# Moving compressed outputs, copies, splits and block sums in the engines' orders of an attention layer

## The chip, the cores and the metric

The kernel runs on one core of a Trainium2 chip. The metric is the device time of one execution in microseconds (us), the median of several. Engines are named as in the profile: PE (TensorE), DVE (VectorE), ACT (ScalarE), POOL (GpSimd), SP (the queue that issues the transfers).

## What is computed

A decoder trunk of two layers over 256 tokens of width 2048, all in float32. Layer 0 mixes with a gated convolution and a gated delta rule. Layer 1, where the change lies, is a sparse attention with 16 query heads in 4 groups of key and value heads:

```python
q, k_c, v_c, k_s, v_s, k_w, v_w, gates = _split_cols(x @ w_in, NSA_WIDTHS)
k_cmp = compress_blocks(kv_heads(k_c), cmp_pos_k, cmp_w1_k, cmp_w2_k)   # blocks of 32, stride 16
v_cmp = compress_blocks(kv_heads(v_c), cmp_pos_v, cmp_w1_v, cmp_w2_v)   # gelu(blocks @ w1) @ w2
...
o = gt[..., 0:1] * o_cmp + gt[..., 1:2] * o_slc + gt[..., 2:3] * o_win
return o @ w_out
```

With 256 tokens there are 15 compressed blocks per group, the selected blocks are all blocks, and the window holds all earlier tokens. Each of the three branches is a softmax over its own keys. After each mixer and each feed-forward network (SwiGLU) comes a layer norm of the scaled residual.

## The kernel before

**Weights.** A float32 product is made of three passes of a reduced type: high by high, high by low and low by high (`passes`, lines 1856 to 1858). So every piece of weights is loaded (`raw`), copied and rounded on ACT (`w_hi`, line 640), subtracted on DVE (`w_lo`, line 1134) and then used by PE. A piece of 128x1024 is called a half. `halves(n)` on ACT and on DVE does the next n of them. There are 4 slots (`HL_SLOTS`): ACT can write half h only after PE has used half h-4, DVE follows ACT, and PE follows DVE. ACT, DVE and PE each run a list of work written out by hand, in which `halves` and the other work alternate; each engine takes its list strictly in order.

**Compressing stage.** PE computes the projections `kc` (8 halves), `gates` (2), `vc` (8), then `w1` for keys (8) and for values (8). Per half PE needs some 2.9 us in the projections and 1.45 us in `w1`. ACT copies the projection out of PSUM into `kcT` (line 983). DVE builds the 32-token blocks with the position embedding (`block_sum(b)`, 8 additions, line 1648), rounds them (`block_hi`, line 1652) and subtracts (`block_lo`, line 1655); PE multiplies them by `w1`. DVE also reduces the rotary angles (lines 1628 to 1636) and mirrors the tables (1671, 1672).

**Attention stage.** For each group g (0 to 3) and token tile t (0, 1) PE does `scores` (one block of 15 columns per head, line 2309, and the selected and window scores, line 2318), `probs_T` (transposes the probabilities, line 2083), `outputs` (the compressed outputs `co`, line 2336, then `po` for the two other branches, line 2345) and `heads_out` (transposes the merged heads, name `oT`). In between `fill(n)` does n halves of the next query projection, or, once those are used up, of the output projection (`out_halves`, whose left side is made by `early_split` on ACT, line 659, and DVE, line 1164). `queries(g)` transposes the rotated queries (line 2278).

ACT does `exps` (lines 1031, 1038), the copies of the transposed probabilities in `probs_T` (1046, 1051), `rope_stage` (1009) and `heads_out` (866). DVE does `rope` (1699 to 1704), `put_T` (copies transposed queries, 1710), the masked scores and their maxima in `scores` (1737 to 1751), `masked`, `weights`, and `branches` (weighs and sums co and po out of PSUM, 1776 and 1778).

**PSUM banks.** All these small results share banks 4 to 7. `K[name]` numbers the uses in the order in which they are listed by `uses`, and the bank is `4 + K[name] % 4`. Before PE writes use k, it waits until the use k-4 has been read:

```python
            def sp_use(name, i=None, per=0):
                k = K[name]
                if k >= 4:
                    pe.wait_ge(sp_free[k % 4], at(k // 4, i, per // 4))
                return bank[4 + k % 4]
```

The read that frees `co` and each `po` is that of DVE in `branches`; the one that frees the queries' banks is `put_T`; the transposed probabilities and `oT` are freed by ACT.

Of the kernel before, what the change touches and what calls it, by code (L numbers as in the profile page):

```python
# [77 lines left out]
def trunk(nc, x_in, positions, ln_mix_g, ln_mix_b, ln_ffn_g, ln_ffn_b, ffn_w_in, ffn_w_out,  # L78
# [6 lines left out]
    with ctx:  # L85
# [172 lines left out]
        hT_ready = sem("hT_ready")  # L258
        bank_whole, xT_ready, yt_by_act, yt_by_dve = sem("bank_whole"), sem("xT_ready"), sem("yt_by_act"), sem("yt_by_dve")
# [46 lines left out]
        def outputs_use(g, t):  # L306
            uses([("co", g, t)] + [("po", g, t, b) for b in range(2)])
# [3 lines left out]
        for g in range(NG):  # L311
            scores_use(g, 1)
            if g:
                uses([("oT", g - 1, 1)])
            probs_use(g, 0)
            outputs_use(g, 0)
            uses([("oT", g, 0)])
            probs_use(g, 1)
            if g < NG - 1:
                uses([("q", 2 * g + 2 + a) for a in range(2)])  # L320
                scores_use(g + 1, 0)
            outputs_use(g, 1)
# [302 lines left out]
        def _(act):  # L625
# [342 lines left out]

            halves(3)
            keep_values(0, C["vs"])  # L970
            for n, kv in enumerate(("kc", "vc")):
                if n:
                    halves(2)
                    c = C["gates"]
                    act.activation(gates_out, chunk_in(c)[0][:, 0:SEQ], ACT.Copy).then_inc(pair_free[c % 2], 1)
                halves(8)
                if n:
                    wait_sp(act, ("gates",))
                    act.activation(gates, last_cols(("gates",), 3 * NH), ACT.Sigmoid).then_inc(sp_free[K[("gates",)] % 4], 1)
                c = C[kv]  # L980
                b = chunk_in(c)
                for a in range(2):
                    ins = act.activation(kcT[:, n, 2 * a:2 * a + 2, :], b[a][:, :].rearrange("p (f t) -> p f t", f=2), ACT.Copy)
                ins.then_inc(pair_free[c % 2], 1)
                if n == 0:
                    rotary_tables()
# [7 lines left out]
            for b in range(2):  # L994
                if b:
                    halves(3)
                    put_hT(("kh",))
                    halves(5)
                else:
                    halves(8)  # L1000
                c = C["w1"] + b
                sums = chunk_in(c)[0][0:NCG, 0:CMPH]
                act.activation(cmp_h[0:NCG], sums, ACT.Gelu_apprx_tanh).then_inc(pair_free[c % 2], 1)
# [58 lines left out]
            for g in range(NG):  # L1062
                exps(g, 1)
                halves(1)
                if g:
                    heads_out(g - 1, 1)
                probs_T(g, 0)
# [5 lines left out]
                if g < NG - 1:  # L1073
                    rope_stage(C["q"] + g + 1, FA[("rope", g)])
                if g == NG - 2:
                    for kt in range(4):
                        early_split("out1", kt)
                heads_out(g, 0)
                halves(1)
                probs_T(g, 1)  # L1080
                if g == NG - 2:
                    for kt in range(4, 8):
                        early_split("out1", kt)
                halves(1)
                if g < NG - 1:
                    exps(g + 1, 0)
                halves(2)
# [12 lines left out]
        def _(dv):  # L1100
# [521 lines left out]
            halves(1)  # L1622
# [3 lines left out]
            for r, n in rows:  # L1626
# [10 lines left out]
                if n.start == 0:  # L1637
                    own(ins)
            to_act(ins)
            halves(5)  # L1640
            def block_sum(b):

                chunk_staged(C["vc" if b else "kc"])
                for hf in range(2):
                    lo = slice(16 * hf, 16 * hf + 16)
                    for g in range(NG):
                        src = kcT[:, b, g, 16 * hf:16 * hf + 16 * NCMP].rearrange("p (n l) -> p l n", l=16)
                        ins = dv.tensor_tensor(blk_sum[:, lo, g * NCMP:(g + 1) * NCMP], src, over(posT[:, b, lo], NCMP), ALU.add)
                own(ins)

            def block_hi(b):
                own(dv.tensor_copy(blk_hi[b][:, 0:blk_n], yt_flat[:, 0:blk_n]))

            def block_lo(b):
                dv.tensor_tensor(blk_lo[b][:, 0:blk_n], yt_flat[:, 0:blk_n], blk_hi[b][:, 0:blk_n].bitcast(F32), ALU.subtract)\
# [6 lines left out]
            block_sum(0)  # L1662
            block_hi(0)
            block_lo(0)
            halves(2 + 8)
# [7 lines left out]
            block_sum(1)  # L1673
            halves(2)
            block_hi(1)
# [113 lines left out]
            halves(3)  # L1789
            turned_q(0)  # L1790
            scores(0, 0)
# [3 lines left out]
            for g in range(NG):  # L1795
# [8 lines left out]
                halves(2)  # L1804
                if g == NG - 2:
                    for kt in range(2):
                        early_split("out1", kt)
                if g < NG - 1:
                    rope(C["q"] + g + 1)
                if g == NG - 2:  # L1810
                    for kt in range(2, 4):
                        early_split("out1", kt)
                halves(1)
                if g == NG - 2:
                    for kt in range(4, 8):
# [6 lines left out]
                if g < NG - 1:  # L1822
                    masked(g + 1, 0)
                    weights(g + 1, 0)
                halves(2)
# [8 lines left out]
        def _(pe):  # L1834
# [496 lines left out]
            def outputs(g, t):  # L2331
# [5 lines left out]
                sp_done(ins, name)  # L2337
                for br in range(2):
# [42 lines left out]
            for g in range(NG):  # L2381
# [5 lines left out]
                fill(1)  # L2387
                outputs(g, 0)
# [4 lines left out]
                if g < NG - 1:  # L2393
                    queries(g + 1)
                    scores(g + 1, 0)
# [52 lines left out]
```

## Time and profile before

| | us |
|---|---|
| median of 3 runs | 2419.82 (2419.26 to 2423.41) |
| the profiled execution | 2425.94 |
| its span, first to last instruction | 2424.2 |
| PE busy in it | 2368.8 |
| DVE busy | 1563.2 |
| ACT busy | 1126.5 |

The span lies 1.7 us below the profiled execution's own time, and that execution took 6.1 us more than the median of the other runs. A busy PE is counted from matmul to matmul with modelled ends, so its share says little of its rate. The mean granted TensorE clock was 0.995 of full speed. The compressing stage lies at 1264 to 1345 us of the span, the attention stage at 1437 to 1630 us.

### The profile page before, as it was taken

What the parts mean: (1) busy time and instruction counts of PE and PEld (TensorE: products, weight loads), DVE (VectorE), ACT (ScalarE), POOL (GpSimd) and SP (SyncE); (2) the same over time, 40 slices, a digit from 0 to 9 for tenths busy, and PEclk for the clock granted to TensorE, in tenths of its full rate; (3) what the DMA queues carried; (4) which work ended last, traced back from release to release, by engine and by line L of the source; (5) the groups of instructions that cost most, each with busy time, mean ns of one, the idle gap of its engine ahead of it and who ended that gap; (6) DMA issues with size and microseconds to landing.
All of it is one profiled execution on the core that took longest, in us unless ns stands there. A gap on an engine that the chain in (4) does not pass through costs nothing.

```text
span 2424.2 us, 32228 instructions
## 1 busy us (share of the span) xinstructions
PE 2368.8 (98%) x12361; PEld 2028.6 (84%) x12361; DVE 1563.2 (64%) x2101; ACT 1126.5 (46%) x1516; POOL 29.6 (1%) x69
## 2 busy tenths in 40 slices
PE   8999999999999999999999999999999999999998
PEld 8999988778888888888879888787888888888886
DVE  6657775577666666655587666766766666666556
ACT  4345554564444444444465445545444444444443
POOL 1000000100000000000000000000000000000000
PEclk9999999999999999999999999999999999999999
DMA  7555521645555555655545652335555555555553
GB/s 263 191 174 174 172 105 55 257 161 193 198 195 193 190 191 191 225 191 194 196 164 180 241 174 87 102 122 195 176 196 195 189 198 190 190 210 207 192 194 115
DMA packets 180090, 437.99 MB, mean 181 GB/s; under 512 B 7232, under 2 KB 19632, under 8 KB 165920
## 3 DMA queue, kind: packets, MB, share of 16 engines
q1 hardware_dynamic: 177984, 425.75, 50.7%
q0 software_dynamic: 2016, 11.02, 1.2%
q8 instruction: 59, 0.97, 0.2%
q14 instruction: 31, 0.25, 0.0%
HBM read 434.64 MB, written 2.10 MB: 180 GB/s over the span
## 4 chain that ended last, share of the span: by engine, by line
PE 90%; DVE 5%; ACT 3%; issue 1%; DMA 0%; SPq 0%; DVEq 0%; ACTq 0%
PE bank L1856 28%; PE bank L1857 28%; PE bank L1858 28%; PE bank L2108 2%; PE bank L2345 1%; DVE w_lo L1134 1%; ACT w_hi L640 1%; PE bank L2318 1%; PE bank L2083 1%; DVE stats L1211 1%; DVE x L1210 1%; DVE spare_lo L1134 0%; PE bank L2336 0%; ACT yt L714 0%; DVE yt L1234 0%
## 5 line engine op out<-in xcount | busy, mean ns | idle before, releaser
L1134 DVE TENSOR_TENSOR w_lo<-raw,w_hi 128x1024 fp32r<-128x1024 f32 x776 | 944.6, 1224 | 733.7 <-ACT w_hi L640 731.7
L640 ACT ACTIVATE w_hi<-raw 128x1024 fp32r<-128x1024 f32 x776 | 820.0, 1060 | 1075.7 <-PE bank L1858 1066.6
L1856 PE MATMUL bank<-w_hi,xt_hi 128*128 128x512 f32 x1904 | 748.2, 393 | 2.5 <-DVE xt_lo L1242 1.2
L1858 PE MATMUL bank<-w_hi,xt_lo 128*128 128x512 f32 x1904 | 743.2, 390 | 0.0
L1857 PE MATMUL bank<-w_lo,xt_hi 128*128 128x512 f32 x1904 | 743.1, 390 | 0.0
L1856 PEld LDWEIGHTS bank<-w_hi,xt_hi 128*128 128x128 f32 x1904 | 358.9, 188 | 77.1 <-issue 1.9
L1858 PEld LDWEIGHTS bank<-w_hi,xt_lo 128*128 128x128 f32 x1904 | 358.6, 188 | 75.0
L1857 PEld LDWEIGHTS bank<-w_lo,xt_hi 128*128 128x128 f32 x1904 | 359.0, 189 | 73.2
L1856 PE MATMUL bank<-xt_hi,w_hi 128*128 128x256 f32 x928 | 267.4, 288 | 9.8 <-DVE w_lo L1134 9.8
L1856 PE MATMUL bank<-w_hi,a_hi 128*128 128x512 f32 x672 | 261.7, 390 | 2.1 <-DVE a_lo L1184 2.1
L1857 PE MATMUL bank<-xt_lo,w_hi 128*128 128x256 f32 x928 | 263.4, 284 | 0.0
L1858 PE MATMUL bank<-xt_hi,w_lo 128*128 128x256 f32 x928 | 263.3, 284 | 0.0
L1857 PE MATMUL bank<-w_lo,a_hi 128*128 128x512 f32 x672 | 261.5, 389 | 0.0
L1858 PE MATMUL bank<-w_hi,a_lo 128*128 128x512 f32 x672 | 261.5, 389 | 0.0
L1856 PEld LDWEIGHTS bank<-xt_hi,w_hi 128*128 128x128 f32 x928 | 178.9, 193 | 12.2 <-issue 9.6
L1857 PEld LDWEIGHTS bank<-xt_lo,w_hi 128*128 128x128 f32 x928 | 178.9, 193 | 2.0 <-issue 1.9
L1858 PEld LDWEIGHTS bank<-xt_hi,w_lo 128*128 128x128 f32 x928 | 178.9, 193 | 0.0
L1331 DVE STREAM_TRANSPOSE big<-yt 32x256 f32<-32x256 f32 x352 | 153.5, 436 | 10.0
L1856 PEld LDWEIGHTS bank<-w_hi,a_hi 128*128 128x128 f32 x672 | 126.1, 188 | 29.3 <-DVE a_lo L1184 3.0
L1858 PEld LDWEIGHTS bank<-w_hi,a_lo 128*128 128x128 f32 x672 | 126.1, 188 | 26.1
L1857 PEld LDWEIGHTS bank<-w_lo,a_hi 128*128 128x128 f32 x672 | 126.1, 188 | 26.0
L762 ACT ACTIVATE yt<-bank 128x512 f32<-128x512 f32 x44 | 23.9, 596 | 43.5 <-PE bank L1858 43.5
(277 smaller groups left out, 1489.7 us busy)
## 6 DMA issues: line engine op xcount, KB each, us to landing
raw<-in_ffn_w_in_dram SPq DMA_DIRECT2D x176, 1024.0 KB, 4.9
raw<-in_ffn_w_out_dram SPq DMA_DIRECT2D x88, 1024.0 KB, 4.8
raw<-in_hy_w_in_dram SPq DMA_DIRECT2D x53, 1024.0 KB, 4.9
raw<-in_nsa_w_in_dram SPq DMA_DIRECT2D x41, 1024.0 KB, 5.0
raw<-in_hy_w_out_dram SPq DMA_DIRECT2D x16, 1024.0 KB, 4.9
raw<-in_nsa_w_out_dram SPq DMA_DIRECT2D x16, 1024.0 KB, 5.1
raw<-in_hy_w_in_dram SPq DMA_DIRECT2D x8, 512.0 KB, 8.6
raw<-in_cmp_w_k_dram SPq DMA_DIRECT2D x4, 1024.0 KB, 5.8
```

The lines of the kernel that those rows point to most:

```text
L640: act.activation(weights_of(h)[0], half_of(h), ACT.Copy).then_inc(w_hi_ready, 1)
L1134: dv.tensor_tensor(lo, half_of(h), hi.bitcast(F32), ALU.subtract).then_inc(w_lo_ready, 1)
L1210: own(dv.scalar_tensor_tensor(v, v, ALPHA, acc_bank(n, t, c)[:, :], ALU.mult, ALU.add))
L1211: ins = dv.bn_stats(stats[:, t, c, :], v)
L1331: ins = dv.transpose(dst, src)
L1856: pe.matmul(dst, l_hi, r_hi, start=start, stop=False, skip_group_check=shared)
L1857: pe.matmul(dst, l_hi, r_lo, start=False, stop=False, skip_group_check=shared)
L1858: return pe.matmul(dst, l_lo, r_hi, start=False, stop=stop, skip_group_check=shared)
L2083: ins = pe.transpose(b[0:rows, h * P:(h + 1) * P], src, ident[:, :])
L2108: ins = pe.matmul(b[:, h * P:(h + 1) * P], lhs(h), rhs(h), start=True, stop=True)
L2318: ins = pe.matmul(b[:, h * kn:(h + 1) * kn], qT[:, 4 * g + hp * k + h, v], ksT[:, br, g, 0:kn], start=True, stop=True)
L2345: ins = pe.matmul(b[:, h * P:(h + 1) * P], pT_buf[br][:, k, h * P:(h + 1) * P], vs[:, br, k, g * DH:(g + 1) * DH], start=k == 0, stop=k == t)
```

## The change

On PE, `compressed_out` becomes a function of its own. For t = 0 it stays ahead of `outputs`; for t = 1 and g < 3 it is issued after `queries(g + 1)` and ahead of `scores(g + 1, 0)`, and its place in the numbering of bank uses moves with it. On ACT, `probs_T(0, 0)` goes ahead of `exps(0, 1)`, `heads_out(2, 0)` ahead of the early splits, and those come in groups of 2, 2 and 4 instead of 4 and 4, the last after `exps(3, 0)`. ACT takes over the rounding `block_hi` from DVE, with two new semaphores. On DVE, halves are placed earlier around the rotary angles, the queries' copy and the block sums; the sums for the values are cut in two, with a half of weights between; and the early splits move behind `rope` and behind `weights(3, 0)`.

```diff
--- before.py
+++ after.py
@@ -256,6 +256,7 @@
         xt_hi_ready, xt_lo_ready = sem("xt_hi_ready"), sem("xt_lo_ready")
         stage_free, silu_done = sem("stage_free"), sem("silu_done")
         hT_ready = sem("hT_ready")
+        blk_ready, blk_hi_ready = sem("blk_ready"), sem("blk_hi_ready")
         bank_whole, xT_ready, yt_by_act, yt_by_dve = sem("bank_whole"), sem("xT_ready"), sem("yt_by_act"), sem("yt_by_dve")
         ident_ready, out_ready = sem("ident_ready"), sem("out_ready")
         out_by_pool = sem("out_by_pool")
@@ -304,7 +305,7 @@
             uses([("cT", g, t)] + [("pT", g, t, b, k) for b in range(2) for k in range(t + 1)])
 
         def outputs_use(g, t):
-            uses([("co", g, t)] + [("po", g, t, b) for b in range(2)])
+            uses([("co", g, t)] * (t == 0 or g == NG - 1) + [("po", g, t, b) for b in range(2)])
 
         uses([("q", a) for a in range(2)])
         scores_use(0, 0)
@@ -317,7 +318,7 @@
             uses([("oT", g, 0)])
             probs_use(g, 1)
             if g < NG - 1:
-                uses([("q", 2 * g + 2 + a) for a in range(2)])
+                uses([("q", 2 * g + 2 + a) for a in range(2)] + [("co", g, 1)])
                 scores_use(g + 1, 0)
             outputs_use(g, 1)
         uses([("oT", NG - 1, 1)])
@@ -966,11 +967,17 @@
                     ins = act.activation(vs[:, n, t, :], b[t][:, :], ACT.Copy)
                 ins.then_inc(pair_free[c % 2], 1)
 
+            def block_hi(b):
+
+                act.wait_ge(blk_ready, b + 1)
+                act.activation(blk_hi[b][:, 0:blk_n], yt_flat[:, 0:blk_n], ACT.Copy).then_inc(blk_hi_ready, 1)
+
             halves(3)
             keep_values(0, C["vs"])
             for n, kv in enumerate(("kc", "vc")):
                 if n:
                     halves(2)
+                    block_hi(0)
                     c = C["gates"]
                     act.activation(gates_out, chunk_in(c)[0][:, 0:SEQ], ACT.Copy).then_inc(pair_free[c % 2], 1)
                 halves(8)
@@ -997,7 +1004,9 @@
                     put_hT(("kh",))
                     halves(5)
                 else:
-                    halves(8)
+                    halves(3)
+                    block_hi(1)
+                    halves(5)
                 c = C["w1"] + b
                 sums = chunk_in(c)[0][0:NCG, 0:CMPH]
                 act.activation(cmp_h[0:NCG], sums, ACT.Gelu_apprx_tanh).then_inc(pair_free[c % 2], 1)
@@ -1060,11 +1069,15 @@
             exps(0, 0)
             halves(1)
             for g in range(NG):
-                exps(g, 1)
-                halves(1)
                 if g:
+                    exps(g, 1)
+                    halves(1)
                     heads_out(g - 1, 1)
-                probs_T(g, 0)
+                    probs_T(g, 0)
+                else:
+                    probs_T(g, 0)
+                    exps(g, 1)
+                    halves(1)
                 halves(1)
                 if g == NG - 1:
                     for kt in range(8, EARLY["out1"]):
@@ -1072,18 +1085,21 @@
                 halves(2)
                 if g < NG - 1:
                     rope_stage(C["q"] + g + 1, FA[("rope", g)])
+                heads_out(g, 0)
                 if g == NG - 2:
-                    for kt in range(4):
+                    for kt in range(2):
                         early_split("out1", kt)
-                heads_out(g, 0)
                 halves(1)
                 probs_T(g, 1)
                 if g == NG - 2:
-                    for kt in range(4, 8):
+                    for kt in range(2, 4):
                         early_split("out1", kt)
                 halves(1)
                 if g < NG - 1:
                     exps(g + 1, 0)
+                if g == NG - 2:
+                    for kt in range(4, 8):
+                        early_split("out1", kt)
                 halves(2)
             heads_out(NG - 1, 1)
             late_halves("out1", KT)
@@ -1619,7 +1635,7 @@
             for j in range(4):
                 halves(1)
                 residual(1, j)
-            halves(1)
+            halves(3)
 
             dv.wait_ge(nsa_in, 16 * 6)
             rows = [(slice(0, P), slice(0, 2)), (slice(0, NCG), slice(2, 3))]
@@ -1636,22 +1652,23 @@
                 ins = dv.scalar_tensor_tensor(tv, av, -1.0, av, ALU.mult, ALU.max)
                 if n.start == 0:
                     own(ins)
+                    halves(2)
             to_act(ins)
-            halves(5)
-            def block_sum(b):
+            halves(1)
+
+            def block_sum(b, hf):
 
                 chunk_staged(C["vc" if b else "kc"])
-                for hf in range(2):
-                    lo = slice(16 * hf, 16 * hf + 16)
-                    for g in range(NG):
-                        src = kcT[:, b, g, 16 * hf:16 * hf + 16 * NCMP].rearrange("p (n l) -> p l n", l=16)
-                        ins = dv.tensor_tensor(blk_sum[:, lo, g * NCMP:(g + 1) * NCMP], src, over(posT[:, b, lo], NCMP), ALU.add)
-                own(ins)
-
-            def block_hi(b):
-                own(dv.tensor_copy(blk_hi[b][:, 0:blk_n], yt_flat[:, 0:blk_n]))
+                lo = slice(16 * hf, 16 * hf + 16)
+                for g in range(NG):
+                    src = kcT[:, b, g, 16 * hf:16 * hf + 16 * NCMP].rearrange("p (n l) -> p l n", l=16)
+                    ins = dv.tensor_tensor(blk_sum[:, lo, g * NCMP:(g + 1) * NCMP], src, over(posT[:, b, lo], NCMP), ALU.add)
+                if hf:
+                    ins.then_inc(blk_ready, 1)
 
             def block_lo(b):
+
+                dv.wait_ge(blk_hi_ready, b + 1)
                 dv.tensor_tensor(blk_lo[b][:, 0:blk_n], yt_flat[:, 0:blk_n], blk_hi[b][:, 0:blk_n].bitcast(F32), ALU.subtract)\
                   .then_inc(for_pe, 1)
 
@@ -1659,10 +1676,11 @@
             for b in range(2):
                 for v in (blk_hi[b], blk_lo[b]):
                     dv.tensor_scalar(v[:, blk_n:blk_w], ones[:, 0:blk_w - blk_n], 0.0, None, ALU.mult)
-            block_sum(0)
-            block_hi(0)
+            block_sum(0, 0)
+            block_sum(0, 1)
+            halves(2)
             block_lo(0)
-            halves(2 + 8)
+            halves(5)
 
             dv.wait_ge(from_act, 20)
             n_from[0] = 20
@@ -1670,9 +1688,10 @@
             for cv, sv in ((cosb, sinb), (cosc[0:NCG].unsqueeze(1), sinc[0:NCG].unsqueeze(1))):
                 own(dv.tensor_copy(cv[:, :, 0:hd], cv[:, :, hd:]))
                 own(dv.tensor_scalar(sv[:, :, 0:hd], sv[:, :, hd:], -1.0, None, ALU.mult))
-            block_sum(1)
-            halves(2)
-            block_hi(1)
+            halves(4)
+            block_sum(1, 0)
+            halves(1)
+            block_sum(1, 1)
             halves(2)
             block_lo(1)
             halves(4)
@@ -1786,8 +1805,9 @@
             def turned_q(g):
                 put_T(K[("q", 2 * g)], lambda a: qT[:, 4 * g + 2 * a:4 * g + 2 * a + 2, :])
 
-            halves(3)
+            halves(2)
             turned_q(0)
+            halves(1)
             scores(0, 0)
             masked(0, 0)
             weights(0, 0)
@@ -1802,17 +1822,14 @@
                     for kt in range(8, EARLY["out1"]):
                         early_split("out1", kt)
                 halves(2)
+                if g < NG - 1:
+                    rope(C["q"] + g + 1)
                 if g == NG - 2:
                     for kt in range(2):
                         early_split("out1", kt)
-                if g < NG - 1:
-                    rope(C["q"] + g + 1)
+                halves(1)
                 if g == NG - 2:
                     for kt in range(2, 4):
-                        early_split("out1", kt)
-                halves(1)
-                if g == NG - 2:
-                    for kt in range(4, 8):
                         early_split("out1", kt)
                 halves(1)
                 if g < NG - 1:
@@ -1822,6 +1839,9 @@
                 if g < NG - 1:
                     masked(g + 1, 0)
                     weights(g + 1, 0)
+                if g == NG - 2:
+                    for kt in range(4, 8):
+                        early_split("out1", kt)
                 halves(2)
             mark().then_inc(gb_free, 1)
             late_halves("out1", KT)
@@ -2328,13 +2348,15 @@
                         p_ = sc_buf[t][br][:, 0:HPG * kn].rearrange("p (h n) -> p h n", h=HPG)
                         transposes(("pT", g, t, br, k), [p_[:, h, k * P:(k + 1) * P] for h in range(HPG)])
 
-            def outputs(g, t):
+            def compressed_out(g, t):
                 name = ("co", g, t)
                 wait_sp_read(pe, ("cT", g, t))
                 b = sp_use(name)
                 for h in range(HPG):
                     ins = pe.matmul(b[:, h * P:(h + 1) * P], pT_cmp[0:NCMP, h * P:(h + 1) * P], vcmp[0:NCMP, g, :], start=True, stop=True)
                 sp_done(ins, name)
+
+            def outputs(g, t):
                 for br in range(2):
                     name = ("po", g, t, br)
                     for k in range(t + 1):
@@ -2385,6 +2407,7 @@
                 fill(1)
                 probs_T(g, 0)
                 fill(1)
+                compressed_out(g, 0)
                 outputs(g, 0)
                 fill(2)
                 heads_out(g, 0)
@@ -2392,6 +2415,8 @@
                 fill(2)
                 if g < NG - 1:
                     queries(g + 1)
+                compressed_out(g, 1)
+                if g < NG - 1:
                     scores(g + 1, 0)
                 outputs(g, 1)
                 fill(2 if g < NG - 1 else 1)
```

## Rows read from the trace of the kernel before

**Rows 1.** The page, busy time of the engines.

```profile
PE 2368.8 (98%) x12361; PEld 2028.6 (84%) x12361; DVE 1563.2 (64%) x2101; ACT 1126.5 (46%) x1516; POOL 29.6 (1%) x69
```

**Rows 2.** Timeline of PE, compressing stage: start, duration, line, operation, [idle before, releaser].

```profile
1296.48 0.39 PE L1856 MATMUL bank<-xt_hi,w_hi 128*128 128x256 f32 x1 [1.09 <-DVE w_lo L1134]
...
1323.64 0.38 PE L1856 MATMUL bank<-w_hi,blk_hi 128*128 128x256 f32 x1 [2.29 <-DVE w_lo L1134]
...
1331.44 0.39 PE L1856 MATMUL bank<-w_hi,blk_hi 128*128 128x256 f32 x1 [1.20 <-DVE w_lo L1134]
```

**Rows 3.** Timeline of DVE and ACT, compressing stage.

```profile
1287.91 4.00 DVE L1648 TENSOR_TENSOR yt<-big 128x240 f32<-128x240 f32 x8 [1.20 <-ACT big L983]
...
1291.94 1.16 DVE L1652 CAST blk_hi<-yt 128x1920 fp32r<-128x1920 f32 x1
...
1293.13 2.16 DVE L1655 TENSOR_TENSOR blk_lo<-yt,blk_hi 128x1920 fp32r<-128x1920 f32 x1
1295.21 4.62 DVE L1134 TENSOR_TENSOR w_lo<-raw,w_hi 128x1024 fp32r<-128x1024 f32 x4
...
1318.13 2.95 ACT L640 ACTIVATE w_hi<-raw 128x1024 fp32r<-128x1024 f32 x3
```

**Rows 4.** Timeline of PE and DVE around the first two query transposes.

```profile
1446.87 1.03 PE L2309 MATMUL bank<-big 128*128 128x15 f32 x8 [0.68 <-DVE big L1710]
...
1486.17 1.04 PE L2309 MATMUL bank<-big 128*128 128x15 f32 x8 [0.99 <-DVE big L1710]
...
1489.02 1.15 PE L2336 MATMUL bank<-big 15*128 15x128 f32 x8
...
1490.10 3.84 PE L2345 MATMUL bank<-big,gb 128*128 128x128 f32 x32
1490.28 0.69 DVE L1751 TENSOR_REDUCE sm<-gb 128x4 f32<-128x512 f32 x1
...
1490.88 1.12 DVE L1776 TENSOR_SCALAR big<-bank,sm 128x128 f32<-128x128 f32 x4
...
1493.70 0.48 PE L1856 MATMUL bank<-w_hi,xt_hi 128*128 128x512 f32 x1
```

**Rows 5.** Group 0, tile 0: a window (busy time by engine), then the timeline.

```profile
1456.20:1463.40 7.20, 7.20 (x39) 6.02 (x40) 4.86 (x7) 5.46 (x25) 0.00 (x0) 1.00 0.00 0
...
1464.85 1.15 PE L2336 MATMUL bank<-big 15*128 15x128 f32 x8 [0.86 <-ACT big L1046]
...
1466.73 1.23 DVE L1134 TENSOR_TENSOR w_lo<-raw,w_hi 128x1024 fp32r<-128x1024 f32 x1 [1.15 <-ACT w_hi L640]
1467.88 1.12 DVE L1776 TENSOR_SCALAR big<-bank,sm 128x128 f32<-128x128 f32 x4
...
1474.94 1.04 PE L2083 MATMUL bank<-ident,big 128*128 128x128 f32 x8
```

**Rows 6.** Timeline of PE and DVE in group 2, where the early splits lie.

```profile
1566.13 0.68 DVE L1699 TENSOR_TENSOR yt<-yt 128x512 f32<-128x512 f32 x1
...
1566.97 0.63 PE L2083 MATMUL bank<-ident,sc_more 128*128 128x128 f32 x4 [1.23 <-ACT big L866]
...
1568.27 0.72 PE L2083 MATMUL bank<-ident,sc_more 128*128 128x128 f32 x4 [0.68 <-ACT big L1046]
1568.68 0.74 PE L1856 MATMUL bank<-w_hi,xt_hi 128*128 128x512 f32 x1
...
1569.93 0.75 DVE L1164 TENSOR_TENSOR xt_lo<-big,xt_hi 128x256 fp32r<-128x256 f32 x2
```

**Rows 7.** Windows: stretch, length, busy PE, PEld, DVE, ACT, POOL; granted clock, DMA share, GB/s.

```profile
1319.00:1323.00 4.00, 2.35 (x20) 2.14 (x19) 3.97 (x8) 3.14 (x4) 0.00 (x0) 1.00 0.02 4
...
1466.00:1470.00 4.00, 4.00 (x20) 3.86 (x20) 3.23 (x9) 1.65 (x2) 0.00 (x0) 0.57 0.79 266
...
1564.00:1568.00 4.00, 2.37 (x20) 1.87 (x18) 3.12 (x7) 3.97 (x9) 0.00 (x0) 1.00 0.78 262
1568.00:1572.00 4.00, 3.73 (x12) 3.05 (x13) 3.97 (x8) 3.35 (x9) 0.00 (x0) 0.59 0.00 0
```

## The prediction

> **What bounds the kernel now.** I read the page first. PE is busy for 2368.8 of 2424.2 us [rows 1], and DVE and ACT have room over the whole span. So the end is set by PE, and an edit counts by what it does to the moments in which PE stands still. The list of PE's waits, then the timeline of the two stages that are edited, show where these are. In the compressing stage PE waits for low halves three times for more than 1 us [rows 2], and once more, at 1327.1, for 0.4: 5.0 us together. In the attention stage it waits before the scores of each group until DVE has copied the transposed queries: 0.68 us for group 0, 0.99 for group 1 [rows 4], and 0.99 and 1.00 for groups 2 and 3. It waits 0.86 us for ACT ahead of `co` of group 0, tile 0 [rows 5], and 0.67 us in groups 0 and 1, 1.91 in group 2 [rows 6] and 0.35 in group 3 in the middle of `probs_T(g, 1)`. That is 12 us of standing still in all that the change can work on, 0.5% of the time. Outside these stages nothing is edited.
>
> The second thing to see is the granted clock. It falls to 1.2 of 2.4 GHz twice in the attention stage: from about 1466.3 and from 1568.7, for some 3.4 us each, in which one matmul of 512 columns follows the other after 0.43 instead of 0.23 us [rows 6, 7]. Before the first lie the wait of 0.86 and matmuls of 15 rows, before the second 1.9 us of waits. So such a spell costs up to 1.7 us of PE's time, beyond the waits themselves.
>
> **Compressing stage, keys.** Before, DVE did 8 sums (4.0 us), `block_hi` (1.16) and `block_lo` (2.16) in one piece and only then the low half for which PE had been waiting for 1.09 us [rows 2, 3]. Now two halves stand between the sums and `block_lo`, `block_hi` is ACT's, and the halves k5 to c0 (half 5 of `kc` to half 0 of `vc`; w and n stand below for those of `w1` of the keys and of the query projections) are done around the angles (about 5.3 us of small instructions, for which DVE has the time: each of these halves is still ready at least 1 us before PE comes to it). The needed half ends at about 1293.2 and PE reaches it at 1295.3: the wait goes, -1.1 us.
>
> **Compressing stage, values.** This is where ACT's new work bites. An ACT copy of 1024 columns takes 0.98 us when the next follows at once [rows 3], so one of 1920 takes 0.98 x 1920 / 1024 = 1.84. I go through the order with PE 1.1 us earlier. ACT copies w3, w4, w5 from 1317.0 to 1320.0, then waits for the second half of the sums. DVE: w3 at 1318.05 (1.155 each, [rows 3]), four sums (2.0) until 1321.2, w4, four sums until 1324.35, w5 until 1325.5. ACT rounds from 1324.4 to 1326.2, and behind it in its queue stands w6, which the order of before had copied at 1321.5: ready at 1327.3. DVE w6 until 1328.45, `block_lo` 2.06 until 1330.5, w7 until 1331.75. PE waits for w4 (0.6), w5 (1.7), w6 (1.5) and w7 (1.7), and starts w7 at 1331.8. Before, it started w7 at 1331.44 [rows 2]. So the 1.1 gained is given back and 0.35 more: **+0.35 for the stage**. From there PE needs 1.45 us a half and DVE 1.16, so no more is lost. Bounds: -1.1 if ACT's copy were no obstacle, +2 if the clock also falls over the four waits; the row at 1319 to 1323, with 2.35 of 4.00 us busy, shows no fall behind it [rows 7], so I leave that out of the sum.
>
> **Start of the heads.** `turned_q(0)` now comes one half earlier and the 0.68 us go: -0.7. `probs_T(0, 0)` on ACT is now ahead of `exps(0, 1)`, so `co` starts without the 0.86. But `exps(0, 1)` (5.46 us of ACT's time in its window, [rows 5], 5.3 if all inputs are there) then ends at about 1466.4 instead of 1463.4, and n15 and n16, the halves behind it, 3.1 us later. DVE has both in front of `branches(0, 0)`. Before, it waited 1.15 us between the two [rows 5]; that slack goes and the branches start at 1469.7 instead of 1467.88. They end 3.45 us later, 1473.2, and only then can PE transpose the heads. Before, PE did that at 1474.94. PE itself would be there at 1471.6, without the wait and with the full clock; it stands still for 1.7 us. Result: 1473.3, which is -1.65 with the -0.7 in it, and -0.1 from the next wait: **-1.75 us**. Bounds: -0.7 (the rest lost, by a fall of the clock) to -3.3 (no wait for the branches).
>
> **Compressed outputs, three times.** Before, `co` (4 products, 1.08 us) followed the scores; now it stands in the 0.99 us for which PE waits for the copied queries. That by itself would be worth 0.99 each. But its bank use moves too. In the new order the uses are q, q, co, c, s, s, po, po: `co` is number i+2, and the first `po` is number i+6, the same bank. The first `po` may therefore be written only after DVE has read `co`, and DVE's list has that behind all of `scores(g + 1, 0)`: the last maximum at 1490.28, the four products by the weights 1490.88 to 1492.00 [rows 4]. These times depend on the copied queries and the scores, which are not earlier than before, since c must still wait for `put_T` until 1486.17. In the order of before the bank of the first `po` was that of c, free since 1487.5, and PE started it at 1490.10. Now it starts at 1492.05, after standing still from 1489.0: +1.95 net of the gap filled, and the 3.6 us of po, the weights halves and all that follows on PE move with it [rows 4]. Three groups: **+5.85 us**. Bounds: -3.0 (if the bank did not bind) to +5.9.
>
> **Early splits in group 2.** Counting from the start of PE's `heads_out(2, 0)`, ACT now frees the oT bank first, so the wait of 1.23 goes; then two splits (0.66) and a half (0.98) delay the copy of the compressed probabilities, and the wait of 0.68 becomes 1.3. DVE does `rope` first, 3.8 us (1566.13 to 1569.93, [rows 6]), and the splits that the next fill needs end at 5.6 us from that start, where PE began the fill at 4.85 (1568.68). So +0.75 if the clock falls again, and -0.85 if it does not, because the fill then takes 5.6 instead of 7.2 us: I take **+0.3**. The four splits moved behind `weights(3, 0)` feed fills that PE reaches more than 5 us later; they cost nothing, and would cost DVE's 1.4 us if that cover were gone. The order of `rope` ahead of them hides behind PE's fill.
>
> **The clock.** Each of the three new waits keeps PE idle for 3.0 us at a stretch, more than the 1.9 us before the fall at 1568.7 [rows 7]. I expect a fall behind two of the three, at up to 1.7 us, the price that the rows show: **+3.3 us**, with 0 and 5 as bounds. The Trainium skill speaks against this term: its page "TensorE: Matmul & The Clock Gate", section "HAM oscillation", warns only of idle gaps longer than any stall in this sum. By that rule the term would be 0 and the time 2424.6. The rows of this kernel show the clock falling behind shorter ones.
>
> **Sum.** 0.35 - 1.75 + 5.85 + 0.3 + 3.3 = +8.1 us. The profiled execution would go from 2425.9 to 2434.0; it lies 6.1 above the median, and I take the change alone to the median: 2419.8 + 8.1 = 2427.9 us. A measurement of this kernel can tell about 0.2% (4.8 us) from no change.
>
> **Rivals.**
> - *Waits without the clock.* The po waits are there, but the clock holds or falls elsewhere: 8.1 - 3.3 = +4.8, 2424.6, on the edge of slower. For it: 0.86 us of waiting was enough once [rows 5], but 2.3 us at 1321.4 were not [rows 2, 7], so the fall depends on more than the length of the wait. Against it: 3.0 us is longer than either.
> - *The compressing stage costs more.* Four waits within 10 us, together 5.5, bring the clock down there too, and ACT is later with w6 and w7 by more than I count: +2 instead of +0.35, and the heads' clock term at its full 5: 8.1 + 1.7 + 1.7 = +11.5, 2431.3.
> - *The bank does not bind; not slower.* If DVE comes to `co` before PE comes to `po`, the move does what it looks like: 3 x 0.99 gained instead of 5.85 lost, and no new clock spells. -1.75 + 0.35 + 0.3 - 3.0 = -4.1, 2415.7. It decides at the point where DVE's read ends before 1490.1; in the rows it ends at 1492.0, so DVE's chain from the queries would have to be 1.9 us shorter. Nothing in the list shortens it.
>
> **Chances.** Forecast 0.5, waits without the clock 0.2, dearer compressing stage 0.15, bank not binding 0.15. The range 2418.5 to 2433.0 reaches over the first three with the bounds of the unknown terms and leaves out most of the last. Slower by over 0.2%: 0.5 + 0.15 + half of 0.2 = 0.75. Within 0.2%: the other half and 0.12 of the last, 0.22. Faster: 0.03. The likeliest case's own range is 2425 to 2431.
>
> **What would show it.** In the profile after, PE's wait ahead of L2309 is gone in groups 0 to 3, and one of about 3 us ahead of L2345, released by DVE L1776, stands in groups 0 to 2. PE's wait at 1295 is gone, and four waits for `w_lo` stand in `w1` of the keys, with ACT's 1920-column copy of 1.8 us ahead of w6's. `heads_out(0, 0)` waits 1 to 2 us for DVE. The clock shows more low spells than two in the attention stage. I am wrong if the wait ahead of L2345 is short, or if the profile shows it and the time does not follow.

## The result and the profile after

The changed kernel takes 2432.74 us (median of 6 runs, 2431.43 to 2434.15), the kernel before 2421.61 beside it. The ratio is 1.0044, 95% interval 1.0031 to 1.0056: about 10.7 us slower. The forecast was +8.1 us, 2427.9 us, with a range of 2418.5 to 2433.0. So the measured time lies only 0.3 us inside the range and above the 2425 to 2431 of the likeliest case. Of the 4.8 us by which it misses 2427.9, 1.8 are the kernel before, which was at 2419.8 in the forecast. One execution of the kernel with the early read (below) took 8458 us at a full clock, where the ten others took 2416.9 to 2423.3; it was left out of that kernel's ratio as slow, and its cause is not known.

The page of the changed kernel, busy time of the engines:

```profile
PE 2369.9 (97%) x12361; PEld 2030.3 (83%) x12361; DVE 1560.2 (64%) x2099; ACT 1129.4 (46%) x1518; POOL 30.6 (1%) x69
```

PE's busy time is what it was [rows 1]; the span is 2432.4 instead of 2424.2 us. Some of PE's waits in the changed kernel, from the list of waits of its whole span (engine, line, releaser: us, times, longest):

```profile
PE bank L2367 <- DVE big L1795: 9.2, 3, 3.1
...
PE bank L2103 <- ACT big L1055: 2.7, 4, 1.3
...
PE bank L2103 <- DVE sm L1135: 1.4, 1, 1.4
PE bank L1876 <- DVE xt_lo L1180: 1.3, 1, 1.3
```

L2367 is the product `po` (L2345 before), L1795 the weighing of `co` by DVE (1776 before). PE's wait for the copied queries (3.6 us in all, [rows 4]) has left the list. The first line is new: 9.2 us in three waits that the kernel before did not have.

The clock differs from execution to execution, outside the edited stages too. In the profile of before it fell three times ahead of 1263 us, in this one once, and the changed kernel is 2.3 us earlier at the start of `kc`, though nothing is edited ahead of it. So stages are best compared from the first product of `kc` (1263.56 before, 1261.31 after). Times from there, read from PE's timelines:

| from the first product of `kc` to | before | after | difference | added since the row above |
|---|---|---|---|---|
| half w7 of `w1`, keys | 67.88 | 67.85 | -0.03 | -0.03 |
| `heads_out(0, 0)` | 211.38 | 209.40 | -1.98 | -1.95 |
| `queries(1)` | 220.59 | 218.14 | -2.45 | -0.47 |
| `queries(2)` | 265.05 | 266.25 | +1.20 | +3.65 |
| `queries(3)` | 312.30 | 317.97 | +5.67 | +4.47 |
| the last `co` | 356.39 | 366.86 | +10.47 | +4.80 |

**The first of the three new waits**, timeline of PE and DVE:

```profile
1480.41 1.15 PE L2356 MATMUL bank<-big 15*128 15x128 f32 x8
...
1481.50 1.06 PE L2329 MATMUL bank<-big 128*128 128x15 f32 x8
...
1485.63 0.69 DVE L1770 TENSOR_REDUCE sm<-gb 128x4 f32<-128x512 f32 x1
...
1486.23 1.12 DVE L1795 TENSOR_SCALAR big<-bank,sm 128x128 f32<-128x128 f32 x4
...
1487.50 5.40 PE L2367 MATMUL bank<-big,gb 128*128 128x128 f32 x32 [3.06 <-DVE big L1795]
...
1492.65 0.48 PE L1876 MATMUL bank<-w_hi,xt_hi 128*128 128x512 f32 x1
```

`co` stands at 1480.41, in the place where PE used to wait, and the scores follow it without a gap. Then PE stands for 3.06 us until the four products on `co` have ended (1487.35). Before, `po` began 3.93 us after the scores' first product (1486.17 to 1490.10, [rows 4]); now it begins 6.00 after it. Counted from the query transposes it is 8.05 us (1479.45 to 1487.50) instead of 5.95 (1484.15 to 1490.10), so the wait costs 2.1 us net of the gap filled. And its 32 products take 5.40 us instead of 3.84. The windows say why (stretch, length, busy PE, PEld, DVE, ACT, POOL, clock, DMA share, GB/s):

```profile
1484.00:1488.00 4.00, 0.94 (x6) 0.78 (x6) 3.28 (x8) 3.34 (x18) 0.00 (x0) 0.93 0.00 0
1488.00:1492.00 4.00, 4.00 (x26) 4.00 (x25) 0.77 (x3) 1.16 (x3) 0.00 (x0) 0.64 0.01 4
...
1584.00:1588.00 4.00, 0.95 (x6) 0.79 (x5) 3.11 (x8) 3.34 (x19) 0.00 (x0) 0.80 0.00 0
1588.00:1592.00 4.00, 4.00 (x21) 4.00 (x21) 0.81 (x4) 2.21 (x6) 0.00 (x0) 0.50 0.01 4
```

The first two rows are the first site, the others the third. PE is idle for three quarters of the first stretch and works at 1.2 GHz for most of the second. At the third site the clock falls at 1586.4, still within the wait (1584.3 to 1587.3), stays low for 6.8 us, and `po` takes 6.63 us.

**Compressing stage.** PE's starts after a wait, then ACT and DVE:

```profile
1319.98 0.38 PE L1876 MATMUL bank<-w_hi,blk_hi 128*128 128x256 f32 x1 [0.82 <-DVE w_lo L1150]
...
1323.04 0.38 PE L1876 MATMUL bank<-w_hi,blk_hi 128*128 128x256 f32 x1 [1.39 <-DVE w_lo L1150]
...
1325.95 0.39 PE L1876 MATMUL bank<-w_hi,blk_hi 128*128 128x256 f32 x1 [1.22 <-DVE w_lo L1150]
...
1329.16 0.39 PE L1876 MATMUL bank<-w_hi,blk_hi 128*128 128x256 f32 x1 [1.52 <-DVE w_lo L1150]
```

```profile
1321.89 1.80 ACT L973 ACTIVATE blk_hi<-yt 128x1920 fp32r<-128x1920 f32 x1 [4.41 <-DVE yt L1665]
1323.60 3.89 ACT L641 ACTIVATE w_hi<-raw 128x1024 fp32r<-128x1024 f32 x4
```

```profile
1324.67 1.22 DVE L1150 TENSOR_TENSOR w_lo<-raw,w_hi 128x1024 fp32r<-128x1024 f32 x1 [1.69 <-ACT w_hi L641]
1325.82 2.15 DVE L1672 TENSOR_TENSOR blk_lo<-yt,blk_hi 128x1920 fp32r<-128x1920 f32 x1
```

The wait at 1296 is gone. Four waits stand in `w1` where three stood (1323.6 and 1331.4 [rows 2], and the one at 1327.1). w7, the last half of the keys' `w1`, starts to within 0.03 us when it did, counted from the start of `kc`. ACT waits 4.41 us for the sums with w6 behind it in its list; DVE waits 1.69 us for w6.

**Group 0.** DVE gets its two halves from ACT late, does them in one piece, and PE waits 1.41 us for the branches (the releaser in the last row, L1135, is the small instruction with which DVE marks their end):

```profile
1464.81 2.36 DVE L1150 TENSOR_TENSOR w_lo<-raw,w_hi 128x1024 fp32r<-128x1024 f32 x2 [6.75 <-ACT w_hi L641]
1467.09 1.12 DVE L1795 TENSOR_SCALAR big<-bank,sm 128x128 f32<-128x128 f32 x4
```

```profile
1470.71 1.09 PE L2103 MATMUL bank<-ident,big 128*128 128x128 f32 x8 [1.41 <-DVE sm L1135]
```

**Group 2, early splits.** PE has two waits of 2.6 us together instead of 1.9 [rows 6], the second now ahead of the fill:

```profile
1570.13 0.66 PE L2103 MATMUL bank<-ident,sc_more 128*128 128x128 f32 x4 [1.28 <-ACT big L1055]
...
1572.10 0.47 PE L1876 MATMUL bank<-w_hi,xt_hi 128*128 128x512 f32 x1 [1.31 <-DVE xt_lo L1180]
```

### The profile page after: what moved, and what is told of

Read it like the earlier page. It is cut to its first block, busy times and chain, and to the rows that moved or that the text cites. A ratio compares the mean times of both kernels' runs of the same rounds, so it can differ in the third digit from the quotient of the medians.

```text
span 2432.4 us, 32227 instructions
## 1 busy us (share of the span) xinstructions
PE 2369.9 (97%) x12361; PEld 2030.3 (83%) x12361; DVE 1560.2 (64%) x2099; ACT 1129.4 (46%) x1518; POOL 30.6 (1%) x69
## 4 chain that ended last, share of the span: by engine, by line
PE 90%; DVE 5%; ACT 3%; issue 1%; DMA 0%; SPq 0%; DVEq 0%; ACTq 0%
PE bank L1876 28%; PE bank L1877 28%; PE bank L1878 28%; PE bank L2128 2%; PE bank L2367 1%; DVE w_lo L1150 1%; PE bank L2338 1%; ACT w_hi L641 1%; PE bank L2103 1%; DVE stats L1227 1%; DVE x L1226 1%; DVE spare_lo L1150 0%; ACT yt L715 0%; DVE yt L1250 0%; ACT spare_hi L641 0%
```

## The experiments

My theory: the move of `co` gives its PSUM bank to the first `po`, PE waits for DVE there, and the wait brings the clock down. Its rivals: the new orders on ACT and DVE cost the time; or the waits count and the clock does not. Ratios are to the kernel before on the same chip, with 95% intervals. Its median there was 2423.74 us beside the first four and 2423.51 beside the last four.

### Compressed outputs back in their place

```diff
-            uses([("co", g, t)] * (t == 0 or g == NG - 1) + [("po", g, t, b) for b in range(2)])
+            uses([("co", g, t)] + [("po", g, t, b) for b in range(2)])
...
-                uses([("q", 2 * g + 2 + a) for a in range(2)] + [("co", g, 1)])
+                uses([("q", 2 * g + 2 + a) for a in range(2)])
...
-                compressed_out(g, 1)
                 if g < NG - 1:
                     scores(g + 1, 0)
+                compressed_out(g, 1)
```

> The changed kernel with compressed outputs of tile 1 back in their old place, on PE and in the numbering of bank uses; all else as changed. Bank theory: the three waits of 3.05 us ahead of L2367 and the low clock behind them go, the three waits of about 1 us ahead of the scores come back. In the changed profile these sites cost 3 x 1.95 + 5.8 = 11.6 us, so the time falls by about 11.6 to 1 us below the kernel before (ratio to it 0.9995, 0.998 to 1.001). Rival, that ACT's and DVE's new orders cost the time: it stays near 1.004. Rival, that only the waits count and the low clock would have come anyway: it falls by 6, to 1.002.

Measured: 2421.07 us, ratio 0.9992 (0.9983 to 1.0001). From the waits of this kernel:

```profile
PE bank L2329 <- DVE big L1729: 3.0, 3, 1.0
```

The three waits for the queries are back, the one ahead of `po` is gone, and the clock did not fall once in the two stages. A window over most of the attention stage has it at 1.00:

```profile
1456.00:1620.00 164.00, 155.52 (x936) 133.50 (x934) 112.51 (x235) 91.34 (x256) 0.00 (x0) 1.00 0.30 97
```

So all other edits together are worth between nothing and a small gain. This refutes the rival that ACT's and DVE's orders cost the time, and that the low clock would have come anyway.

### Only the move

The kernel before with the move alone: the lines above the other way round, and `compressed_out` taken out of `outputs`.

> The kernel before with only the move of the compressed outputs of tile 1, on PE and in the numbering. Bank theory: waits of 3.0 us ahead of the first po in groups 0 to 2 and low clock behind them, 3 x 1.95 + 3 x 1.6 = +10.7 us, ratio 1.0044 (1.003 to 1.005). Rival, that ACT's and DVE's orders cost the time: 1.000. Rival, waits alone without the clock: +5.9, 1.0024.

Measured: 2430.27 us, ratio 1.0034 (1.0021 to 1.0047). From its waits:

```profile
PE bank L2347 <- DVE big L1776: 9.2, 3, 3.1
```

The same 9.2 us. The move alone makes most of the loss or all of it. In the profiled execution the clock fell behind only one of the three waits, so the low clock is likely, not certain. Its attention stage has two low spells, as many as that of before, and from the first product of `kc` to the last `co` it takes 362.38 us against 356.39: the 6.0 us more are the three waits, net of the gaps filled.

This profile also answers a reading of the prediction, that the wait of 2.3 us in `w1` was not enough for a fall [rows 2, 7]. The same wait, with nothing edited ahead of it, had one here:

```profile
1320.00:1324.00 4.00, 2.02 (x9) 2.03 (x10) 3.96 (x5) 0.84 (x1) 0.00 (x0) 0.70 0.20 34
```

It cost nothing: w7 starts 67.88 us after the first product of `kc` in both profiles, because DVE sets the pace there, and PE's waits of 0.38 and 1.20 us behind it shrank to a single one of 0.54.

### DVE reads the compressed outputs early

```diff
                     turned_q(g + 1)
+                    branches(g, 1, (0,))
                     scores(g + 1, 0)
-                branches(g, 1)
+                branches(g, 1, (1, 2) if g < NG - 1 else (0, 1, 2))
```

The third argument of `branches` chooses which of `co` and the two `po` it weighs. PE's order and the banks are those of the changed kernel.

> The changed kernel, but in groups 0 to 2 DVE weighs the compressed outputs of tile 1 straight after the copy of the queries, ahead of the next scores, so that the bank is free when PE comes to it. Bank theory: neither the waits of 3.05 us nor those of 1 us ahead of the scores stand, and no low clock behind them: about 11.6 + 3 x 0.99 = 14.6 us below the changed kernel, some 3.9 below the kernel before, ratio 0.998 (0.997 to 1.000). The maxima come 1.1 us later; if the exponentials are the bound, the gain is smaller by up to 3. Rival, that what costs is the place of co on PE and not its bank: 1.003 to 1.004, as changed.

Measured: 2417.94 us, ratio 0.9978 (0.9969 to 0.9988), faster than both kernels. Timeline at the first site:

```profile
1480.01 1.15 PE L2360 MATMUL bank<-big 15*128 15x128 f32 x8
...
1481.27 1.13 DVE L1797 TENSOR_SCALAR big<-bank,sm 128x128 f32<-128x128 f32 x4 [0.31 <-PE bank L2360]
...
1482.01 2.03 PE L2342 MATMUL bank<-big 128*128 128x128 f32 x16
...
1483.88 1.84 PE L2371 MATMUL bank<-big,gb 128*128 128x128 f32 x15
```

`co` is read at 1481.3 to 1482.4, and PE goes from the scores into `po` without a gap. Where `co` stands on PE costs nothing; the late read of its bank does. The maxima stand behind this read on DVE, as expected, and no wait on PE has grown by it. From the first product of `kc` to the last `co` it takes 351.15 us, 2.1 less than with `co` back in its place (353.28), although the clock fell once here, in group 2, and not there. By the totals the two intervals overlap.

### PE kept busy during the wait

```diff
             def outputs(g, t):
+                if t and g < NG - 1:
+                    b = sp_use(("po", g, t, 1))
+                    for _ in range(11):
+                        pe.matmul(b[:, :], xt_hi[:, 13, 0:P], xt_hi[:, 14:16, :].rearrange("p k n -> p (k n)"), start=True, stop=True)
```

The extra products add nothing to the output: the second `po` overwrites them.

> The changed kernel, and in each of the three waits PE does 11 extra matmuls of 512 columns on old data (2.5 us, results unused) into the bank of the second po. The waits stay, but PE is busy in them. If the low clock behind the waits is a cost of its own, it goes: 3 x 1.4 to 1.9 us = 4.2 to 5.8 below the changed kernel, ratio to before 1.0022 (1.0015 to 1.003). If the clock does not follow the waits, the time stays as changed, 1.0044, or more where the extra matmuls outlast the wait.

Measured: 2428.17 us, ratio 1.0016 (1.0007 to 1.0025): 0.28% below the changed kernel's ratio, some 6.8 us (an estimate, as the two were not measured together), though PE has 33 products more to do. Timeline and windows at the first site:

```profile
1484.23 2.79 PE L2363 MATMUL bank<-xt_hi 128*128 128x512 f32 x11
```

```profile
1484.00:1488.00 4.00, 3.49 (x20) 2.69 (x19) 3.32 (x8) 3.34 (x19) 0.00 (x0) 1.00 0.00 0
1488.00:1492.00 4.00, 4.00 (x34) 3.87 (x34) 1.67 (x7) 1.21 (x3) 0.00 (x0) 1.00 0.02 4
```

The bank is still free only at 1487.5, but the clock stays at 2.4 GHz behind it, here and at both other sites. From the first product of `kc` to the last `co` this kernel takes 360.95 us and the changed one 366.86, 5.9 us more. So the low clock is a cost of its own, in this pair of profiles about as large as the waits.

### The exponentials first again

```diff
+                exps(g, 1)
+                halves(1)
                 if g:
-                    exps(g, 1)
-                    halves(1)
                     heads_out(g - 1, 1)
-                    probs_T(g, 0)
-                else:
-                    probs_T(g, 0)
-                    exps(g, 1)
-                    halves(1)
+                probs_T(g, 0)
```

> The changed kernel with ACT's order of before in group 0: the exponentials of tile 1 ahead of the copies of tile 0's transposed probabilities. The exchange theory (the wait of 0.86 us taken away came back as 1.4 us ahead of heads_out): the wait ahead of co is back with 0.86, the one of 1.4 us goes. From the first query scores to heads_out(0, 0) PE takes 0.1 to 0.5 us less than changed if the clock holds, 1.2 us more if it falls as it did before. Total within 0.1% of changed, ratio to before 1.0035 to 1.005. Rival, that the exchange was a clean gain of 0.86 or more: 1 to 2 us slower than changed with a full clock.

Measured: 2433.23 us, ratio 1.0043 (1.0029 to 1.0056); the total does not tell it from the changed kernel. Its profile has the old wait back and none ahead of `heads_out(0, 0)`:

```profile
1461.77 1.15 PE L2352 MATMUL bank<-big 15*128 15x128 f32 x8 [0.88 <-ACT big L1055]
```

`heads_out(0, 0)` comes 210.44 us after the first product of `kc`, against 209.40 in the changed kernel. The clock fell here behind the wait of 0.88, as in the profile of before. So the exchange is worth 1.0 us in these executions. By these two waits alone it would lose 0.5, for 0.88 went and 1.41 came; the gain is that of a low spell that the changed kernel did not have there.

### One more half ahead of ACT's rounding

```diff
-                    halves(3)
+                    halves(4)
                     block_hi(1)
-                    halves(5)
+                    halves(4)
```

> The changed kernel with one more half of weights (w6) on ACT ahead of its rounding of the values' block sums. Queue theory (w6 stood behind the rounding): the four waits of 0.8, 1.4, 1.2 and 1.5 us in w1 of the keys shrink by about 1.2 us in sum or more, w7 starts 1.2 to 1.9 us earlier. Rival, that DVE's own work is the bound there: no difference in the start of w7 (within 0.2 us). In the total 0.05 to 0.08% below changed, hardly measurable; the profile decides.

Measured: 2430.67 us, ratio 1.0035 (1.0021 to 1.0048), in the total too close to the changed kernel to tell. PE's starts after a wait in `w1` of the keys:

```profile
1319.89 0.39 PE L1876 MATMUL bank<-w_hi,blk_hi 128*128 128x256 f32 x1 [0.83 <-DVE w_lo L1150]
...
1322.94 0.38 PE L1876 MATMUL bank<-w_hi,blk_hi 128*128 128x256 f32 x1 [1.39 <-DVE w_lo L1150]
...
1327.28 0.39 PE L1876 MATMUL bank<-w_hi,blk_hi 128*128 128x256 f32 x1 [1.25 <-DVE w_lo L1150]
```

Three waits instead of four, and w7 at 66.07 us after the first product of `kc` instead of 67.85: 1.8 us for one half moved, and `queries(1)` is still 1.8 us earlier (216.34 against 218.14). The gain of the first sums was given back in ACT's queue, as the forecast had it.

### Two halves ahead of the exponentials, with the early read

```diff
                 else:
                     probs_T(g, 0)
+                    halves(2)
                     exps(g, 1)
-                    halves(1)
-                halves(1)
+                if g:
+                    halves(1)
```

> The kernel with the early read of the compressed outputs, and in group 0 the two halves of weights on ACT ahead of the exponentials of tile 1. If the 1.4 us wait ahead of heads_out(0, 0) comes through these halves to DVE's branches, it goes, and the time falls by 1.4 us against the kernel with the early read alone: ratio to before 0.9972 (0.996 to 0.998). If the exponentials themselves are what is late, the wait stays or moves to the transposes of tile 1's probabilities and the time stays at 0.9978.

Measured: 2416.16 us, ratio 0.9972 (0.9962 to 0.9982). `heads_out(0, 0)` starts 207.80 us after the first product of `kc` (209.42 with the early read alone), and its row shows no idle time before it (the totals of the two kernels are too close to tell them apart):

```profile
1468.94 1.04 PE L2108 MATMUL bank<-ident,big 128*128 128x128 f32 x8
```

The wait of 1.41 came through the halves, not through the exponentials. A part of the gain goes again a little later: the wait for ACT in `probs_T(0, 1)` is 0.67 us instead of 0.36.

### All mends together

Early read, `halves(2)` ahead of `exps(0, 1)`, w6 ahead of the rounding, and:

```diff
                     for kt in range(2):
                         early_split("out1", kt)
+                probs_T(g, 1)
                 halves(1)
-                probs_T(g, 1)
```

on ACT; on DVE the first two early splits go back ahead of `rope`.

> All the mends together: early read of co, halves ahead of the exponentials in group 0, w6 ahead of the rounding, ACT's copies of tile 1's probabilities ahead of the next half in all groups, and in group 2 DVE's two early splits ahead of rope as before. Theory: the waits of 0.36, 0.67, 1.28 + 1.31 and 0.35 in the middle of probs_T(g, 1) fall to under 1 us together, w7 comes 1.2 us or more earlier, the 1.4 goes: 1.4 + 1.2 + 2.5 = 5 us below the kernel with the early read, ratio to before 0.9957 (0.994 to 0.997). Rival, that the half put behind probs_T is missed by PE: a wait for w_lo after the queries, and 0.997 to 0.998.

Measured: 2409.36 us, ratio 0.9944 (0.9930 to 0.9957): 0.56% faster than the kernel before, and about 1.0% below the changed one by the two ratios. All that is left of the waits in the middle of `probs_T` is in this line of its waits:

```profile
PE bank L2108 <- ACT big L1055: 0.3, 1, 0.3
```

From the first product of `kc` to the last `co` it takes 341.88 us, against 356.39 before and 366.86 changed; no half of weights is missed behind the queries, and in the attention stage the clock did not fall. Against the early read alone that is 9.3 us by the profiles (8.2 by the ratios), where 5 were expected; 1.6 of it, an estimate from the price of a spell, is the low spell that the profile with the early read had in group 2 and this one has not. The mends were not tried one by one here, so their shares stay open.

## Why the prediction was right

- **Compressing stage, forecast +0.35.** Right in mechanism: the first wait went and the queue behind ACT's rounding gave it back. Measured -0.03. ACT's copy of 1920 columns took 1.80 us (1.84 in the forecast), and four sums 2.0. The run with w6 ahead of the rounding shows that this queue was the cause. The clock did not fall in this stage.
- **Start of the heads, -1.75.** Measured -2.42 (-2.45 in the table, of which -0.03 is the stage before). The wait for the branches came, with 1.41 us where 1.7 was foreseen, and the wait after it shrank from 0.67 to 0.35 where I had taken 0.1 off. DVE began the branches 205.78 us after the first product of `kc` (1467.09), where I had counted 206.14 (1469.7).
- **The po waits, +5.85.** Three waits of 3.06, 3.05 and 3.05, foreseen as 3.0, with the releaser named; net of the gap filled 2.1 each, 6.3, instead of 1.95. The move alone reproduces them, and the early read takes them away together with the loss. Rival "the bank does not bind" is refuted.
- **Early splits, +0.3.** Measured +1.0 (4.47 between the queries of groups 2 and 3, less 2.1 and 1.41 at the second site): waits of 1.28 and 1.31 instead of 1.23 and 0.68, and the clock low in both profiles. I had taken a middle between +0.75 and -0.85; the case with the clock was the one that came, and that is luck of the execution. With the compressed outputs back the clock held, and from `queries(2)` to `queries(3)` that kernel took 46.70 us against 47.25 before, 0.55 less.
- **The clock, +3.3.** In this profile it is the term furthest off: `po` took 5.40, 5.25 and 6.63 us against 3.84, so 1.56 + 1.41 + 2.79 = 5.8 us, above the 5 that I had as a bound. I had expected two falls, and none of twice the length. Rival "waits without the clock" is refuted by the run with the busy PE, whose 2.8 us of products in each wait brought 5.9 us back. Over more profiles the term is better than that. Four were taken with these waits and an idle PE; this is what the 32 products of `po` took at each site (us):

  | kernel | first site | second | third | above 3 x 3.84 |
  |---|---|---|---|---|
  | changed | 5.40 | 5.25 | 6.63 | 5.8 |
  | only the move | 3.81 | 5.25 | 3.81 | 1.4 |
  | exponentials first | 6.57 | 5.44 | 3.81 | 4.4 |
  | one more half | 3.81 | 5.44 | 5.16 | 3.0 |
  | PE kept busy, for comparison | 3.81 | 3.81 | 3.81 | none |

  The clock fell behind 8 of 12 waits, two of three as forecast, and the price is 3.6 us on average (sites at 3.81 counted as nothing). The changed kernel's profile had more falls and more cost than the other three, and its execution was the longest of its six. The rule of the Trainium skill, page "TensorE: Matmul & The Clock Gate", section "HAM oscillation", that long idle gaps are what costs the clock, would have had the change at +4.8. The traces show the clock falling behind gaps of 3.06 us and of 0.88.
- **Rival "the compressing stage costs more".** Its 2431.3 lies nearest to the measured time, but half of its reason did not come: the stage measured -0.03 where this rival has +2. Only its clock term of 5 did, in this profile.
- **A sum in the prediction.** The waits that it lists add to 13.1 us, not 12 (5.0 + 3.6 + 0.9 + 2.4 + 1.2). Nothing in the forecast rests on it.

The terms as measured add to -0.03 - 2.42 + 6.3 + 1.0 + 5.8 = 10.6, against 10.5 between the two profiles from the start of `kc` and 10.7 by the ratio. That the profiles and the ratio agree so well is in part chance, because the low spells differ from execution to execution. The forecast of +8.1 was low by the clock, above all (2.5 us in this profile), with 0.7 from the splits and 0.45 from the po waits; against these the first two terms came out 1.05 us better than forecast. Without that offset the measured time would lie outside the range, so the number owes something to luck, and the mechanism does not. What remains open is when a spell comes and how long it is: 6.8 us at the third site here and at the first in the run with the exponentials first, 3.4 or none elsewhere.

## What to carry to other kernels

When a product moves in an order that numbers its buffers in turn, find who gets its buffer next and when the old content is read: here a gap of 0.99 us was filled and one of 3.05 opened, though no engine got more work. Mend the reader before undoing the move. And where a copy is handed to another engine, look at what stands behind it in that engine's queue while it waits: one half ahead of it was worth 1.8 us.

## What the runs showed of the hardware

- Eleven products of 512 columns in a wait of 3 us held the granted clock at 1.00 at all three sites, where the same wait with an idle PE brought it to 1.2 of 2.4 GHz behind 8 of 12. With this useless work the kernel was 5.9 us faster from `kc` to the last `co`, profile against profile.
- The clock also fell behind a wait of only 0.86 to 0.88 us followed by products of 15 rows, in three of the three profiled executions that had that wait, and there in none of the seven that had the same products without it.
- What a low spell costs depends on who sets the pace. Over the products of `po` one of 3.4 us cost up to 1.6 us and one of 6.8 up to 2.8. The one in `w1` of the kernel with only the move cost nothing, since PE was waiting for DVE there anyway.
- Spells of low clock come in 3.4 and 6.8 us here, and their number outside the edited stages varied from one to three between executions of kernels that are the same there: `kc` began between 1260.88 and 1264.02 us of the span, 3.1 us of difference in a single profile that no edit explains.
